# A fifth buffer for expert weights, used once, in a fused two-block kernel on one Trainium2 core

## The reference

```python
h = h + mixed @ w_out[l]
h = h + hier_moe(rms_norm_2(h, norm2_gain[l]), ...)   # per token, two experts e:
    hdn = jax.nn.silu(xblk @ w_gate[e]) * (xblk @ w_up[e])    # 1024 -> 512
    yb  = hdn @ w_down[e]                                     # 512 -> 1024
return rms_norm_2(h, final_norm_gain)
```

## Time and profile before

| | |
|---|---|
| median of three executions | 1078.68 us |
| profiled execution | 1082.16 us |
| its span, first to last instruction | 1080.4 us |
| PE busy | 917.2 us, 85% |
| DVE busy | 444.5 us, 41% |
| ACT busy | 316.9 us, 29% |
| HBM read | 290.76 MB |
| mean granted TensorE clock | 0.955 of full speed |

### The profile page before, as it was taken

The page is one execution under the profiler, slowest core; times in us unless marked ns, Lnnn a source line. Parts: engine busy times, 40 slices in busy tenths (PEclk is TensorE's granted clock), DMA queues, the critical chain, the costliest instruction groups (busy, mean ns, idle before and its releaser), DMA issues.

```text
span 1080.4 us, 18085 instructions
## 1 busy us (share of the span) xinstructions
PE 917.2 (85%) x7830; PEld 654.0 (61%) x7830; DVE 444.5 (41%) x556; ACT 316.9 (29%) x400; POOL 19.0 (2%) x36
## 2 busy tenths in 40 slices
PE   5989999999999999999998978676867777587755
PEld 5989998999999878999988723131312213131311
DVE  4577777676656448995756401010100001010102
ACT  4346675454344327544422300000000000000001
POOL 1300000000000000000000100000000000000000
PEclk9998999999999999999988999898998989988999
DMA  9993244445654454442035789999999999999994
GB/s 337 259 333 115 79 157 156 156 157 158 209 180 170 181 195 157 157 158 78 4 120 211 317 363 421 421 421 422 422 422 421 422 422 422 422 422 422 422 421 189
DMA packets 83395, 294.90 MB, mean 273 GB/s; under 512 B 5887, under 2 KB 33167, under 8 KB 58624
## 3 DMA queue, kind: packets, MB, share of 16 engines
q1 hardware_dynamic: 78240, 284.18, 67.7%
q10 hardware_dynamic: 3552, 6.07, 1.6%
q0 software_dynamic: 1536, 3.68, 1.2%
HBM read 290.76 MB, written 4.10 MB: 273 GB/s over the span
## 4 chain that ended last, share of the span: by engine, by line
PE 54%; DMA 32%; DVE 6%; SPq 4%; ACT 2%; issue 1%; DVEq 0%; ACTq 0%
DMA arena<-in_w_down 17%; PE psum L930 13%; PE psum L932 13%; PE psum L931 13%; DMA arena<-in_w_up 11%; SPq L791 4%; PE psum L1453 3%; PE psum L1250 3%; DMA arena<-in_w_gate 3%; DVE ring_rounded L1909 1%; PE psum L1473 1%; PE psum L905 1%; PE psum L897 1%; PE psum L1442 1%; PE psum L1500 1%
## 5 line engine op out<-in xcount | busy, mean ns | idle before, releaser
L1453 PE MATMUL psum<-arena,featL 128*32 128x512 f32 x1024 | 171.3, 656 | 66.0 <-DMA arena<-in_w_up 51.4
L1909 DVE TENSOR_TENSOR ring_rounded<-arena,hi_rounded 128x2048 fp32r<-128x2048 f32 x77 | 175.9, 2289 | 98.3 <-ACT hi_rounded L1555 97.2
L1555 ACT ACTIVATE hi_rounded<-arena 128x2048 fp32r<-128x2048 f32 x77 | 146.6, 1912 | 161.2 <-PE psum L932 62.3
L930 PE MATMUL psum<-hi_rounded,featT_rounded 128*128 128x256 f32 (+1 forms) x560 | 167.4, 299 | 6.6 <-DVE featL_rounded L1925 3.9
L931 PE MATMUL psum<-ring_rounded,featT_rounded 128*128 128x256 f32 (+1 forms) x560 | 164.8, 294 | 0.0
L932 PE MATMUL psum<-hi_rounded,featL_rounded 128*128 128x256 f32 (+1 forms) x560 | 164.8, 294 | 0.0
L1453 PEld LDWEIGHTS psum<-arena,featL 128*32 128x32 f32 x1024 | 39.4, 118 | 191.6 <-DMA arena<-in_w_up 90.2
L1473 PE MATMUL psum<-arena 128*32 128x512 f32 x512 | 101.5, 701 | 46.8 <-DMA arena<-in_w_down 41.0
L930 PEld LDWEIGHTS psum<-hi_rounded,featT_rounded 128*128 128x128 f32 x560 | 110.6, 197 | 10.0 <-DVE ring_rounded L1909 4.2
L931 PEld LDWEIGHTS psum<-ring_rounded,featT_rounded 128*128 128x128 f32 x560 | 110.6, 197 | 1.2
L932 PEld LDWEIGHTS psum<-hi_rounded,featL_rounded 128*128 128x128 f32 x560 | 110.4, 197 | 1.3
(11 more groups left out here) (281 smaller groups left out, 1143.1 us busy)
## 6 DMA issues: line engine op xcount, KB each, us to landing
arena<-in_w_gate SPq DMA_DIRECT2D x75, 1024.0 KB, 26.5
arena<-in_w_up SPq DMA_DIRECT2D x75, 1024.0 KB, 26.6
arena<-in_w_down SPq DMA_DIRECT2D x65, 1024.0 KB, 26.7
arena<-in_w_in SPq DMA_DIRECT2D x14, 2048.0 KB, 9.0
arena<-in_w_down SPq DMA_DIRECT2D x5, 2048.0 KB, 7.7
arena<-in_w_out SPq DMA_DIRECT2D x4, 2048.0 KB, 8.8
arena<-in_w_in SPq DMA_DIRECT2D x4, 1024.0 KB, 9.6
t_copies<-arena ACTq DMA_DIRECT2D x1, 2048.0 KB, 7.2
```

What stands on the lines that cost most here:

```text
L930: mm(o, lhs[0], rhs[0], start=start, stop=False, skip_group_check=True)
L1453: ins = mm(psum[32 * j:32 * j + 32, MB[4 + m], :], xg[:, 4 * half + k, 32 * j:32 * j + 32], quad[quad_slot(q)][:, j, 512 * k:512 * k + 512 ...
L1555: fn(high, view, ACT.Copy).then_inc(hi_ready, 1)
L1909: tt(low, view, high.bitcast(F32), ALU.subtract).then_inc(lo_ready, 1)
```

## The change

A fifth buffer is added for one use: set 4 is loaded into it ahead of the experts. Two of its pieces lie in `cst`, which is laid out anew so that what the experts need (`ident`, `slot`, `desc`, `before`, `ones`) comes first, and all from `reset` on, with `lora`, `gup`, `tanh_w` and `sig_g` behind it, can be overwritten. The other two lie in the arena behind the ring, so the experts' small tiles (`G`, `Gw`, `GT`, `sg`, `h`, `hT`) move into `featT`, with `hT` over `sg`, and the last norm's gain into `rows`. Pieces 0 and 1 wait for `mat Ark 1` emptied, piece 2 for `mixed_ready` 4, piece 3 for `logit 1`. From set 5 on the ring of four goes on, shifted by one set: set 5 takes the buffer of set 0. For that the first pair is written out in straight code on SP and PE, and the loops run over the other three.

```diff
-LE = layout(("G", 256), ("Gw", 256), ("GT", 256), ("sg", 512), ("h", 512), ("hT", 512), base=NQ * QUAD)
-ARENA = max(L1["end"], LM["end"], LE["end"])
+LE = layout(("G", 256), ("Gw", 256), ("GT", 256), ("sg", 512), ("h", 512))
+ARENA = max(L1["end"], LM["end"], NQ * QUAD + SLOT)
...
+CST = layout(("ident", 128), ("slot", CAP), ("desc", 8), ("before", 128), ("ones", 128), ("gap", 24),
+             ("reset", T), ("winm", 64), ("wina", 64),
...
+HELD = layout(("lora", 512), ("gup", 512), ("tanh", T), ("gate", T), base=CST["end"])
+SPENT = CST["reset"][0]
+assert HELD["end"] - SPENT >= SLOT
...
         quad = [piece(QUAD * n, EG, 4 * 512) for n in range(NQ)]
+        quad = [[q[:, j] for j in range(EG)] for q in quad]
+        quad.append([cst[:, SPENT + 2048 * j:SPENT + 2048 * (j + 1)] for j in range(2)]
+                    + [arena[:, NQ * QUAD + 2048 * j:NQ * QUAD + 2048 * (j + 1)] for j in range(2)])
...
+        spent = featT[:].rearrange("p a b -> p (a b)")
+        G, Gw = (area(LE, n, NT, EG, CAP, of=spent) for n in ("G", "Gw"))
+        GT = area(LE, "GT", NT, P, of=spent)
+        sg, hh = (spent[:, LE[n][0]:LE[n][1]] for n in ("sg", "h"))
+        hhT = area(LE, "sg", 4, P, of=spent)
+        final_gain = rows[:, ROWS["ret_gn"][0]:ROWS["ret_gn"][0] + D]
...
-        def quad_slot(q):
-            return (2, 3, 1, 0)[q % NQ]
+        PLACES = (2, 3, 1, 0)
+
+        def quad_place(r, pair, q):
+
+            if not isinstance(r, int):
+                return PLACES[q % NQ]
+            if isinstance(pair, int) and pair * 12 + q <= NQ:
+                return (*PLACES, NQ)[q]
+            return PLACES[(q - 1) % NQ]
+
+        def quad_level(r, pair, q):
+
+            if not isinstance(r, int):
+                less = 16 if quad_place(r, pair, q) == PLACES[-1] else 0
+                return r * (12 * 16) + pair * (3 * 16) + (q // NQ + 1) * 16 - less
+            if isinstance(pair, int) and pair * 12 + q <= NQ:
+                return 16
+            return pair * (3 * 16) + ((q - 1) // NQ + 1) * 16
...
                 if first:
                     sp.wait_ge(mixed_ready, NT)
-                    load_quad(0, 0, pieces=(1, 2, 3))
+                    load_quad(0, 0, 0, pieces=(1, 2, 3))
+                    wait_emptied(sp, "mat", "Ark", 1)
+                    load_quad(0, 0, NQ, pieces=(0, 1))
                     for key, pieces in RELEASED:
                         wait_filled(sp, *key)
                         for q, k in pieces:
-                            load_quad(0, q, pieces=(k,))
+                            load_quad(0, 0, q, pieces=(k,))
                     sp.wait_ge(mixed_ready, 2 * NT)
+                    load_quad(0, 0, NQ, pieces=(2,))
...
-                    load_quad(0, 3)
+                    load_quad(0, 0, 3)
+                    wait_filled(sp, "logit", NT - 1)
+                    load_quad(0, 0, NQ, pieces=(3,))
+                    for q in range(NQ + 1, 12):
+                        load_quad(0, 0, q, 4 * (q - NQ - (q <= 2 * NQ)))
+                    with sp.Fori(1, NG // 2) as pair:
+                        for q in range(12):
+                            load_quad(0, pair, q, pair * 48 + 4 * (q - NQ))
...
-            nc.gpsimd.dma_start(featT[:, 0:4, :].rearrange("p a b -> p (a b)"),
-                                A["final_gain"].to_broadcast([P, D])).then_inc(gain_in, 16)
+            nc.gpsimd.dma_start(final_gain, A["final_gain"].to_broadcast([P, D])).then_inc(gain_in, 16)
...
             def moe_round(r):
-                with pe.Fori(0, NG // 2) as pair:
+                if isinstance(r, int):
+                    for gp in range(2):
+                        moe_group(r, 0, gp)
+                with pe.Fori(1 if isinstance(r, int) else 0, NG // 2) as pair:
                     for gp in range(2):
                         moe_group(r, pair, gp)
```

More of the change, by code:

```diff
@@ L359, in build @@
         featL, featLR = sb_rounded("featL", [P, DK, T])
-        cst = sb("cst", [P, CST["end"]])
+        cst = sb("cst", [P, HELD["end"]])
+        lora, gup, sig_g = (cst[:, slice(*HELD[n])] for n in ("lora", "gup", "gate"))
+        tanh_w = cst[0:64, slice(*HELD["tanh"])]
         cols = sb("cols", [P, COLS["end"]])
         rows = sb("rows", [P, ROWS["end"]])
-        lora = sb("lora", [P, 512])
-        gup = sb("gup", [P, 512])
         wr = sb("wr", [P, DK, 36])
@@ L412, in build @@
         warm = sb("warm", [P, 1])
-        tanh_w = sb("tanh_w", [64, T])
-        sig_g = sb("sig_g", [P, T])
         prob = area(L1, "prob", 2, 2, 2, T)
@@ L532, in build @@
         count_ready = sem("count_ready")
-        quad_in = [[sem(f"quad_in{n}_{k}") for k in range(4)] for n in range(NQ)]
+        quad_in = [[sem(f"quad_in{n}_{k}") for k in range(4)] for n in range(NQ + 1)]
         pieces_read = sem("pieces_read")
@@ L777, in _, with load_quad @@
                     nc.sync.dma_start(piece((n % NSLOT) * SLOT + off, k, w), src).then_inc(slot_in[n % NSLOT], 16)
-            def load_quad(pair, q, read=None, pieces=range(4)):
+            def load_quad(r, pair, q, read=None, pieces=range(4)):
                 gp, q6 = q // QUADS_PER_GROUP, q % QUADS_PER_GROUP
@@ L790, in load_quad @@
                         sp.wait_ge(pieces_read, read + (j + 1))
-                    nc.sync.dma_start(quad[quad_slot(q)][:, j], w[:, j, 2048 * half:2048 * half + 2048])\
-                        .then_inc(quad_in[quad_slot(q)][j], 16)
+                    at = quad_place(r, pair, q)
+                    nc.sync.dma_start(quad[at][j], w[:, j, 2048 * half:2048 * half + 2048]).then_inc(quad_in[at][j], 16)
             def moe_stream(r, first):
@@ L811, in moe_stream @@
                     for q in range(NQ):
[L812 to L817, removed]
+                        load_quad(r, 0, q)
+                    with sp.Fori(0, NG // 2 - 1) as pair:
+                        for q in range(NQ, 12 + NQ):
+                            load_quad(r, pair + q // 12, q % 12, r * (4 * ALLQ) + pair * 48 + 4 * (q - NQ))
+                    for q in range(NQ, 12):
+                        load_quad(r, NG // 2 - 1, q, r * (4 * ALLQ) + 4 * (ALLQ - 12 + q - NQ))
             moe_stream(0, True)
@@ L1431, in moe_group @@
                 base = r * (4 * ALLQ) + pair * 48 + gp * 24
+                place = lambda q: quad_place(r, pair, q)
                 def expert_ready(q, j):
-                    pe.wait_ge(quad_in[quad_slot(q)][j], r * (12 * 16) + pair * (3 * 16) + (q // NQ + 1) * 16)
+                    pe.wait_ge(quad_in[place(q)][j], quad_level(r, pair, q))
                 pe.wait_ge(onehot_ready, n + 1)
@@ L1453, in moe_group @@
                                 ins = mm(psum[32 * j:32 * j + 32, MB[4 + m], :], xg[:, 4 * half + k, 32 * j:32 * j + 32],
-                                         quad[quad_slot(q)][:, j, 512 * k:512 * k + 512], start=half == 0 and k == 0,
+                                         quad[place(q)][j][:, 512 * k:512 * k + 512], start=half == 0 and k == 0,
                                          stop=half == 1 and k == 3, skip_group_check=True)
@@ L1473, in down @@
                     return mm(psum[32 * j:32 * j + 32, MB[4 + half], :], hhT[:, k, 32 * j:32 * j + 32],
-                              quad[quad_slot(q)][:, j, at_:at_ + 512], start=k == 0, stop=k == 3, skip_group_check=True)
+                              quad[place(q)][j][:, at_:at_ + 512], start=k == 0, stop=k == 3, skip_group_check=True)
                 q = 6 * gp + 4
```

21 lines of the change are left out of this document (7 added, 14 removed).

## The result

The changed kernel takes 1068.0 us (median, 1067.31 to 1070.17), the kernel before 1078.99 us in the same measurement: 10.99 us less, ratio 0.9901 with a 95% interval of 0.9889 to 0.9914, which is 9.3 to 12.0 us. Forecast were 10.2 us less and 1068.5 us.

The account below looks back on a forecast made before the run. From about 624 us the weight pieces still to move were taken to set the end, 2.486 us each. Four hidden pieces (-9.94) and the start (-0.3) gave -10.2, from 1078.68 to 1068.5 us; own range 1067.2 to 1070.2, with rivals 1067.0 to 1071.4.

Parts of the forecast that it names:

- The sum: Whole kernel: 9.94 us less for four hidden pieces and 0.3 less at the stream's start, 10.2 us less.
- (d): Start of the weight stream: first load issued by straight code, not a loop pass; 0.3 us gain, bounds 0 and 0.5.
- (a) to (c): Set 4's four pieces, loaded ahead of the experts, hide in idle DMA gaps between 560 and 624 us; 2.486 us each.
- rival B: Ahead of the stream: one piece, most likely piece 3, isn't hidden and costs 2.5 us; 1071.0 us, chance 0.06.
- (e): Ring of four in the stream: 14.0 us of PE work at worst against 29.8 us queued; zero cost.
- (f): SP's and PE's later loop entry: 4.07 us at the loop's turn, covered by ten queued pieces; zero cost.
- (g): Experts' small tiles moved: same instructions, same shapes; zero cost, bounded by 0.69 us a group.
- (h): More DMA beside the critical work at 560 to 592 us: DVE's operations stay at 0.69 us; zero cost.
- Rival C: At SP's or PE's loop entry the ring runs dry once, 34 us needed to lose; 1080.9 us, chance 0.03.
- (i): Tail after 1065.35 us: unchanged at 15.05 us, zero taken; last 26 matmul records could add up to 2.98 us.
- rival A: In the tail: the end falls into the low clock, adding 2.9 us; 1071.4 us, chance 0.07.
- Rival D: Whole kernel: the change does nothing, since something other than bytes, such as PE, sets the end; 1078.7 us, chance 0.02.

Follow-up runs that it names:

- the second measurement: The changed kernel measured again, nothing altered, against the kernel before: 1070.53 us against 1080.12, ratio 0.9908.
- the second profile: The changed kernel, nothing altered, profiled again; 436.34 us from PE's first matmul on set 0 to its start on the last piece to land.
- Half of the set late: Changed kernel with pieces 2 and 3 of set 4 issued only when set 0 has been read: 1075.64 us, ratio 0.9974 to the kernel before.
- The straight pair alone: Kernel before with only the first pair written out on SP and PE, no fifth buffer, ring unshifted: 1080.07 us against 1080.12, ratio 0.9993.
- ring of two: Changed kernel where from set 9 on a load waits for the set two earlier, not four: 1068.67 us, ratio 0.9911 to the kernel before.
- Set 4 late: Changed kernel with all of set 4 loaded only when set 0's pieces have been read: 1079.46 us against 1080.12 before, ratio 0.9993.

## Why the prediction was right, by its own steps

**The sum.** Four pieces hidden, 9.94 us. P to L went from 446.25 to 436.22 and 436.34, 10.03 and 9.91 us; 174 pieces lie between, and 176 pieces with everything else of the change in place give 446.16. This is the one thing that the change does, shown from both sides: take the early transfers away and the gain goes, take the bytes away without the change and it comes. That the first median lies within 0.5 us of the forecast is finer than these runs measure, and in part luck: the interval of the gain is 9.3 to 12.0 us, the second measurement gave 9.6, and of the 10.2 forecast 0.3 are not there (d).

**(a) to (c), the four covers.** Right. In the second profile, whose times can be laid beside the forecast's, SP issues the new pieces at 551.96 to 553.11, at 581.64 and at 607.49, where 551.8 to 552.8, 581.7 and 607.5 were forecast, and the engines' shares are as forecast (above). In the first profile SP's third issue for set 0 ends at 547.06 + 2.17 = 549.23, and the first new one follows at 549.27. The DVE row that the wait between them looks for:

```profile
546.95 1.41 DVE L2268 TENSOR_TENSOR arena<-psum,cst 128x512 f32<-128x512 f32 x2
```

ends at 548.36, so the wait was met when SP came to it. Half of the set late cost half of the gain in the trace, so pieces 2 and 3 are hidden too; rival B is out.

**(d), the start.** The 0.3 us (bounds 0 and 0.5) was mis-sized and in the sum worth nothing. From P to S the straight code gains 0.47 to 0.56 us in every kernel that has it, about the upper bound. But it does not reach the end: S to L less 2.486 a piece is 4.50 us before and 4.91 to 5.23 in the six profiles with straight code, full pieces and nothing added (172, 174 or 176 of them). The straight pair alone gives a ratio of 0.9993. More than half of it is gone before a byte moves: the first packet starts 0.64 us behind S in the kernel before and 0.97 us behind it with straight code, so it comes only 0.23 us sooner behind P. By 14 us behind S both have moved 5.2 MB. Why the first packet is later, and where the rest goes, is open.

**(e), the ring.** The conclusion (cost zero) was right and the arithmetic behind it was wrong. It set 14.0 us, a down set's matmuls and scatter and gather, against three queued sets; by that a ring of two should run dry at every change of group, and it doesn't. The scatter and the gather run while the next set is landing anyway. The load that waits for group n's last set needs only that set's own matmuls, 3.6 to 6.6 us, against the 9.94 us of the set behind it; the load that waits for the next group's first set has that set's 9.94 us to run in as well. This is worked out from durations; what is measured is that the ring of two loses nothing. So after the start two buffers are enough in this kernel, and the other three serve only to hold what is loaded ahead.

**(f), (g), (h).** No cost is seen. Set 4 late (ratio 0.9993) bounds (f) and (g) together at -0.22% to +0.08%; it has no early transfers and says nothing on (h). That is shown by the second profile: with the four pieces moved beside it, the stretch ahead takes 69.08 us, before 69.06, at the same granted clock of 0.88.

(f) came out at zero as forecast, but it misread its row. The 6.00 us at 726.76 are not the loop's turn. The load issued there is the fourth of its pass; the turn lies ahead of the issue at 722.37, where SP goes 0.80 us between two issues instead of 0.16 (0.70 and 0.66 us at the loop's two turns in the changed kernel). Rows of about 6 us come at every eighth load, with eleven or twelve loads outstanding, and in straight code too: one of 6.28 us starts at 650.90 in the changed kernel, whose loop begins at 666.5. In the ring of two, which turns the same loop with a shorter queue, they are gone but for one at 631.32, from before the queue shortens. SP's issues of `in_w_gate`, with the shortest, median and longest in ns, of the changed kernel and of the ring of two:

```profile
L814 SPq DMA_DIRECT2D arena<-in_w_gate x56: 328/1916/5995, 620.9 to 982.4; - x56
L814 SPq DMA_DIRECT2D arena<-in_w_gate x56: 327/333/595, 621.9 to 997.0; - x56
```

So the 4.07 us are no stall at a branch: at the turns themselves no more than 0.64 us can be one. The long rows go with the length of the queue. Rival C would have needed 34 us and stood on this reading; the rate shows no dip.

**(i), the tail, and rival A.** The last 26 records took 4.08 us here and 3.62 in the second profile of the same kernel; over thirteen profiles they go from 3.55 to 6.53, and the tail with them from 14.8 to 17.6. So a tail longer than 15.05 us, which the prediction named as a sign of being wrong, did show in the first profile (15.64 us), and not in the second (14.82). Rival A is real as a thing that happens to single executions and is part of the spread, but it isn't what the change does: the medians of both kernels may mix it.

**Rival D** is out, with bytes left out in two places and P to L following.

The Trainium skill's "SBUF — State Buffer", section "The DMA setup-cost knee", has a fixed cost of about 2 us a transfer, most of it the confirmation that the last byte is there. The trace doesn't bear out so much at the one place where nothing hides it, the end of the stream. The changed kernel's windows there:

```profile
1047.00:1048.00 1.00, 0.38 (x1) 0.18 (x2) 0.00 (x0) 0.00 (x0) 0.00 (x0) 0.81 0.55 229
1048.50:1049.50 1.00, 1.00 (x2) 0.00 (x0) 0.00 (x0) 0.00 (x0) 0.00 (x0) 0.50 0.06 25
```

The 16 engines run out one after another: a share of 0.06 is one of them. The last packet ends at 1049.56, and PE starts on the last piece at 1050.06, 0.50 us later.

## What to carry to other kernels

When a phase is bound by transfers, as this one is, count the bytes that are left when the stream can no longer pause, and look for gaps ahead of it: a piece moved in a gap was worth its full time at the plateau's rate here, and depth of buffering beyond what kept the queue from running dry was worth nothing else. Before a long row is put down to a loop's turn, look whether it comes at the turns. Leave out or delay the bytes alone to test such a claim, and look at what the edit itself puts into the stream. Before two spans are compared, cut both at places that the change can't move: 4.7 of the 14.7 us between these two profiles had nothing to do with it.

## What the runs showed of the hardware that was not expected

**The clock ahead of the experts comes in more than one pattern, for the same kernel.** "Ahead" took from 64.40 to 69.19 us with the same work on PE, and in two profiles of the same changed kernel 66.78 and 69.08 us. The windows at the same offsets from S0 (8 and 24 us behind it), of the changed kernel's first profile, of its second, and of the straight pair alone:

```profile
555.06:563.06 8.00, 7.63 (x175) 6.99 (x175) 3.57 (x8) 1.15 (x3) 0.00 (x0) 0.79 0.89 368
571.06:579.06 8.00, 7.17 (x43) 7.08 (x43) 5.64 (x9) 2.70 (x3) 0.00 (x0) 0.65 0.98 380
```

```profile
558.06:566.06 8.00, 7.85 (x147) 7.47 (x144) 3.34 (x6) 1.14 (x3) 0.00 (x0) 0.53 0.80 330
574.06:582.06 8.00, 6.44 (x33) 6.26 (x34) 7.21 (x13) 3.19 (x4) 0.00 (x0) 0.61 1.01 422
```

```profile
556.63:564.63 8.00, 7.41 (x227) 6.65 (x227) 4.79 (x11) 1.52 (x4) 0.00 (x0) 1.00 0.35 126
572.63:580.63 8.00, 8.00 (x58) 8.00 (x59) 4.49 (x8) 2.57 (x3) 0.00 (x0) 0.83 0.62 260
```

The granted clock is 0.53 and 0.61 where "ahead" is 69.08 us, 0.79 and 0.65 at 66.78, 1.00 and 0.83 at 64.91: parts of these stretches are at 1.2 GHz. The more of it, the longer, in the thirteen profiles together: the mean granted clock of "ahead" is 0.97 at 64.40 us, 0.95 at 64.91 and 66.75, 0.92 at 66.52 and 66.78, 0.90 at 67.65, and 0.88 at 68.81 to 69.19. What PE does ahead of such a part is the recurrence's small matmuls, with waits for DVE between them, as in the kernel before:

```profile
557.01 0.80 PE L1284 MATMUL psum<-arena 64*64 64x64 f32 x10 [1.08 <-DVE arena L2308]
```

P to L repeats within 0.12 us in the changed kernel's two profiles; it is this stretch, what lies ahead of it, and the tail that spread single executions by several microseconds; what decides the pattern of an execution the runs don't show.
